# Modulation weights in units of 256 rows by 1024 columns, summed in one bank per vector

## What is computed

```python
def ada_mods(cond, w, b):
    mods = (jax.nn.silu(cond) @ w + b)[..., None, :]
    return jnp.split(mods, ADA_CHUNKS, axis=-1)

sh1, sc1, g1, sh2, sc2, g2 = ada_mods(c, ada_w[i], ada_b[i])
u = modulate(rms_norm(x, mix_pre_g[i]), sh1, sc1)
y = pool_mixer(u, pool_w[j], pool_scale[j])
x = x + g1 * rms_norm(y, mix_post_g[i])
f = conv_ffn(modulate(rms_norm(x, ffn_pre_g[i]), sh2, sc2), ...)
x = x + g2 * rms_norm(f, ffn_post_g[i])
```

## Time and profile before

| | us |
|---|---|
| median of 3 runs | 1162.6 (1162.14 to 1165.11) |
| the profiled execution | 1162.76 |
| its span, first to last instruction | 1161.0 |
| PE busy in it | 1144.4 |

### The profile page before, as it was taken

How to read it: one execution, slowest core, us unless ns; L and a number is a source line. 1 busy time by engine, 2 the same in 40 slices (tenths; PEclk the granted TensorE clock), 3 DMA queues, 4 the chain that set the end, 5 groups by cost and what they waited for, 6 DMA issues and landing times.

```text
span 1161.0 us, 17692 instructions
## 1 busy us (share of the span) xinstructions
PE 1144.4 (99%) x7128; PEld 941.7 (81%) x7128; DVE 564.5 (49%) x908; ACT 495.7 (43%) x655; POOL 444.0 (38%) x336
## 2 busy tenths in 40 slices
PE   9899999999999999999999999999999999999997
PEld 7668888888888888888788888888888888888886
DVE  2572654324451245556986657622110344576835
ACT  4474553544421134774433334554421343534531
POOL 0105554545545451433432311033544535465420
PEclk9999999999999999999999999999999999999999
DMA  9994232332242242223223213013242322323201
GB/s 347 384 385 143 79 108 83 99 108 80 100 130 86 96 141 104 83 73 109 73 74 110 73 37 110 1 37 109 73 156 105 113 78 73 110 74 95 89 1 73
DMA packets 104312, 127.74 MB, mean 110 GB/s; under 512 B 13251, under 2 KB 90801, under 8 KB 104117
## 3 DMA queue, kind: packets, MB, share of 16 engines
q1 hardware_dynamic: 99138, 119.62, 31.1%
q10 hardware_dynamic: 5107, 7.16, 1.8%
HBM read 121.53 MB, written 5.24 MB: 109 GB/s over the span
## 4 chain that ended last, share of the span: by engine, by line
PE 93%; DVE 4%; ACT 2%; issue 1%; POOL 0%; DVEq 0%; ACTq 0%; POOLq 0%
PE ps L273 25%; PE ps L275 24%; PE ps L274 24%; PE ps L1715 3%; PE ps L1741 2%; PE ps L2177 1%; PE ps L2258 1%; PE ps L2264 1%; PE ps L1721 1%; PE ps L2259 1%; PE ps L1784 1%; PE ps L1771 1%; PE ps L2240 1%; PE ps L1992 1%; PE ps L2379 1%
## 5 line engine op out<-in xcount | busy, mean ns | idle before, releaser
L407 POOL TENSOR_TENSOR wl<-raw,wh 128x512 fp32r<-128x512 f32 x312 | 422.8, 1387 | 636.6 <-ACT wh L444 636.6
L273 PE MATMUL ps<-xth,wh 128*128 128x512 f32 (+1 forms) x832 | 325.4, 391 | 0.8 <-DVE xtl L1115 0.6
L275 PE MATMUL ps<-xth,wl 128*128 128x512 f32 (+1 forms) x832 | 317.6, 382 | 0.0
L274 PE MATMUL ps<-xtl,wh 128*128 128x512 f32 (+1 forms) x832 | 317.3, 381 | 0.0
L444 ACT ACTIVATE wh<-raw 128x2048 fp32r<-128x2048 f32 x78 | 149.3, 1914 | 299.0 <-PE ps L275 279.4
L273 PEld LDWEIGHTS ps<-xth,wh 128*128 128x128 f32 x832 | 156.5, 188 | 34.4 <-issue 4.8
L275 PEld LDWEIGHTS ps<-xth,wl 128*128 128x128 f32 x832 | 156.4, 188 | 30.7
L274 PEld LDWEIGHTS ps<-xtl,wh 128*128 128x128 f32 x832 | 156.7, 188 | 28.3 <-issue 0.5
L1123 DVE SCALAR_TENSOR_TENSOR conv_out<-ps,conv_taps,conv_out 128x511 f32<-128x511 f32 x44 | 32.7, 744 | 122.6 <-ACT conv_out L609 122.6
L1218 DVE SCALAR_TENSOR_TENSOR conv_v<-ps,gdn_taps,conv_v 128x511 f32<-128x511 f32 (+2 forms) x96 | 71.8, 748 | 28.9 <-ACT conv_v L677 26.2
L273 PE MATMUL ps<-wh,xth 128*128 128x512 f32 x176 | 69.7, 396 | 0.1
(11 more groups left out here) (341 smaller groups left out, 1668.4 us busy)
## 6 DMA issues: line engine op xcount, KB each, us to landing
ada<-in_ada_w SPq DMA_DIRECT2D x24, 1024.0 KB, 10.9
raw<-in_gdn_w_in SPq DMA_DIRECT2D x24, 1024.0 KB, 5.2
raw<-in_ffn_w_up SPq DMA_DIRECT2D x22, 1024.0 KB, 4.9
raw<-in_gla_w_in SPq DMA_DIRECT2D x12, 1024.0 KB, 5.1
raw<-in_ffn_w_down SPq DMA_DIRECT2D x11, 1024.0 KB, 4.8
raw<-in_gdn_w_out SPq DMA_DIRECT2D x8, 1024.0 KB, 4.8
raw<-in_gla_w_out SPq DMA_DIRECT2D x4, 1024.0 KB, 4.9
xres<-in_x SPq DMA_DIRECT2D x4, 512.0 KB, 5.3
```

The lines of the kernel that those rows point to most:

```text
L273: nc.tensor.matmul(o, lh, rh, start=first, stop=False)
L274: nc.tensor.matmul(o, lh, rl, start=False, stop=False)
L275: return nc.tensor.matmul(o, ll, rh, start=False, stop=last)
L407: rest = nc.gpsimd.tensor_tensor(lo[:, part], raw[:, s, part], hi[:, part].bitcast(f32), ALU.subtract)
```

## The change

A unit now holds 256 rows of 1024 columns: `[128 partitions, 2 row blocks, 1024 columns]`, pieces of 4 KB. Each unit adds to all 1024 columns of its vector, so a vector is complete after its fourth unit and not before. PE makes four matmuls of 512 columns for a unit: row block b and column half h go to column group 2b + h, all in one bank, which is j % 2. So partitions 0 and 64 hold the partial sums of the left half, 32 and 96 those of the right half, and `group_rows` gets two columns that select them. One copy of the bank (`ada_sum`) takes the place of two; `ada_part` holds two vectors in turn. For j = 3 ACT makes the only copy. The bias row of j = 2 lies as two rows of 512 on partitions 0 and 32 and needs two short transfers. `gate_sum` makes one step of 1024 columns for each row block, 8 instead of 32. `ada_summed` now counts vectors.

```diff
-    ada = at("ada", PH + 50 * KB, [ADA_SLOTS, KD, UC])
+    ada = at("ada", PH + 50 * KB, [ADA_SLOTS, 2, D])
...
-            ada_v = cols(a["ada_w"][0], UC)
+            ada_v = a["ada_w"][0].rearrange("(n b p) (j c) -> j n p b c", b=2, p=P, c=D)
...
-                nc.gpsimd.memset(group_rows[32 * c:32 * c + 1, :], 1.0).then_inc(S("prepared"), 1)
+                nc.gpsimd.memset(group_rows[32 * c:32 * c + 1, c % 2:c % 2 + 1], 1.0).then_inc(S("prepared"), 1)
...
-            act.dma_start(gate_bias[0:1, :], a["ada_b"][:, 2 * D:3 * D]).then_inc(S("post_in"), 16)
+            for half in range(2):
+                c = 2 * D + half * 512
+                act.dma_start(gate_bias[32 * half:32 * half + 1, 0:512], a["ada_b"][:, c:c + 512]).then_inc(S("post_in"), 16)
...
-            act.wait_ge(S("mod_mm"), 3)
-            act.wait_ge(S("ada_summed"), 7)
+            act.wait_ge(S("mod_mm"), 2)
+            act.wait_ge(S("ada_summed"), 3)
             nc.scalar.activation(ada_part[:, 1, :], ps[:, 1, :], ACT.Copy).then_inc(S("ada_summed"), 1)
...
-            def ada_half(j, half, b):
-
-                v.wait_ge(S("ada_used"), 4 * j + 2 * half + 2)
-                if j >= 1:
-                    v.wait_ge(S("mod_mm"), j)
+            def ada_sum(j):
+
+                v.wait_ge(S("ada_used"), 4 * j + 4)
+                if j >= 2:
+                    v.wait_ge(S("mod_mm"), j - 1)
                 if j == 2:
-                    v.wait_ge(S("post_in"), 16)
-                    V.tensor_tensor(ada_part[:, half, :], ps[:, b + half, :], gate_bias[:, half * 512:half * 512 + 512], ALU.add)\
-                        .then_inc(S("ada_summed"), 1)
+                    v.wait_ge(S("post_in"), 32)
+                    V.tensor_tensor(ada_part[:, j % 2, :], ps[:, j % 2, :], gate_bias[:, 0:512], ALU.add).then_inc(S("ada_summed"), 1)
                 else:
-                    V.tensor_copy(ada_part[:, half, :], ps[:, b + half, :]).then_inc(S("ada_summed"), 1)
+                    if j == 4:
+                        v.wait_ge(S("ada_summed"), 4)
+                    V.tensor_copy(ada_part[:, j % 2, :], ps[:, j % 2, :]).then_inc(S("ada_summed"), 1)
...
-            ada_half(2, 0, 0)
             norm("y", 0)
-            ada_half(2, 1, 0)
+            ada_sum(2)
...
-            ada_half(3, 0, 0)
             norm("y", 3)
...
-            ada_half(4, 0, 0)
             mod_col(3, 2, SH2)
-            ada_half(4, 1, 0)
+            ada_sum(4)
...
-                for n in range(4):
-                    u, part = 20 + n, g2_acc[:, n * UC:(n + 1) * UC]
...
+                V.scalar_tensor_tensor(g2_acc[:], ada[:, u % ADA_SLOTS, k % 2, :], c_col[:, k:k + 1], g2_acc[:], ALU.mult, ALU.add)\
+                    .then_inc(S("g2_summed"), 1)
...
-                if n % 2 == 0 and j >= 1:
-                    pe.wait_ge(S("ada_summed"), 2 * (j - 1) + n // 2 + 1)
-                for k in range(KD):
-                    c = 32 * (k % 4)
-                    mm = X.matmul(ps[c:c + 32, b + n // 2, o], c_col[:, k:k + 1].broadcast_to([P, 32]), ada[:, u % ADA_SLOTS, k, :],
-                                  start=(k < 4), stop=(k >= 4))
+                if n == 0 and j >= 2:
+                    pe.wait_ge(S("ada_summed"), j - 1)
+                for b in range(2):
+                    k = 2 * n + b
+                    for half in range(2):
+                        c = 32 * (2 * b + half)
+                        mm = X.matmul(ps[c:c + 32, j % 2, :], c_col[:, k:k + 1].broadcast_to([P, 32]),
+                                      ada[:, u % ADA_SLOTS, b, half * 512:half * 512 + 512], start=(n == 0), stop=(n == 3))
...
+                pe.wait_ge(S("ada_summed"), j + 1)
                 for half in range(2):
-                    pe.wait_ge(S("ada_summed"), 2 * j + half + 1)
-                    mm = X.matmul(ps[:, b + half, :], group_rows[:, 0:1].broadcast_to([P, P]), ada_part[:, half, :], start=True, stop=True)
+                    mm = X.matmul(ps[:, b + half, :], group_rows[:, half:half + 1].broadcast_to([P, P]), ada_part[:, j % 2, :], start=True, stop=True)
```

More of the change, by code:

```diff
@@ L1153, in gate_sum @@
             def gate_sum(k):
-                for n in range(4):
-                    u, part = 20 + n, g2_acc[:, n * UC:(n + 1) * UC]
[L1157 to L1160, removed]
-                        v.wait_ge(S("g2_summed"), 4 * (k - 1) + n + 1)
-                    V.scalar_tensor_tensor(part, ada[:, u % ADA_SLOTS, k, :], c_col[:, k:k + 1], part, ALU.mult, ALU.add)\
-                        .then_inc(S("g2_summed"), 1)
+                u = 20 + k // 2
+                if k == 0:
+                    v.wait_ge(S("g2_bias"), 16)
+                else:
+                    v.wait_ge(S("g2_summed"), k)
+                if k % 2 == 0:
+                    v.wait_ge(ada_full[u % ADA_SLOTS], 16 * (u // ADA_SLOTS + 1))
+                V.scalar_tensor_tensor(g2_acc[:], ada[:, u % ADA_SLOTS, k % 2, :], c_col[:, k:k + 1], g2_acc[:], ALU.mult, ALU.add)\
+                    .then_inc(S("g2_summed"), 1)
             with v.Fori(0, 2) as i:
@@ L1750, in mod_col @@
                     for c in range(0, P, 32):
-                        mm = X.matmul(ps[c:c + 32, b, n:n + 1], ada_part[:, half, k * P + c:k * P + c + 32], group_rows[:, 0:1],
+                        mm = X.matmul(ps[c:c + 32, b, n:n + 1], ada_part[:, j % 2, k * P + c:k * P + c + 32], group_rows[:, half:half + 1],
                                       start=True, stop=True)
@@ L1824, in _ @@
                 pool_block(cb)
-            ada_unit(0, 2, 0)
-            ada_unit(0, 3, 0)
+            ada_unit(0, 2)
+            ada_unit(0, 3)
             for cb in range(4, KD):
@@ L1837, in _ @@
             mixed(0)
-            ada_unit(2, 0, 0)
-            ada_unit(2, 1, 0)
-            ada_unit(2, 2, 0)
-            ada_unit(2, 3, 0)
+            ada_unit(2, 0)
+            ada_unit(2, 1)
+            ada_unit(2, 2)
+            ada_unit(2, 3)
             pe.wait_ge(S("mods_done"), 2)
@@ L1845, in _ @@
             mixed(2)
-            ada_unit(3, 0, 0)
+            ada_unit(3, 0)
             mixed(3)
-            ada_unit(3, 1, 0)
-            ada_unit(3, 2, 0)
-            ada_unit(3, 3, 0)
+            ada_unit(3, 1)
+            ada_unit(3, 2)
+            ada_unit(3, 3)
             turn_normed(0)
@@ L1888, in _ @@
             pe.wait_ge(S("mods_done"), 5)
-            pe.wait_ge(S("ada_summed"), 10)
+            pe.wait_ge(S("ada_summed"), 5)
             up_units(0)
```

30 lines of the change are left out of this document (14 added, 16 removed).

## The result

The changed kernel takes 1168.35 us (median of 5 runs, 1166.68 to 1169.7), the kernel before 1162.6 (5 runs, 1162.14 to 1165.11): a ratio of 1.0048, interval 1.0036 to 1.0061, 5.7 us slower. The forecast was 1163.4 and the range ended at 1165.9. The profiled execution of the changed kernel took 1167.97 us, 5.2 more than that of before.

A forecast was written before the change was run, and what follows sets the result against it. The prediction took PE to bound the kernel (99% busy), before 87 us by order and latency; terms -0.19, 0, +0.9 and +0.14 sum to +0.85, on 1162.6 giving 1163.4 us, range 1161.2 to 1165.9.

The forecast's parts named there:

- the one on SP: SP's weight stream: fewer descriptors per unit, SP held less, issue still waiting for PE to free a slot; nothing more.
- The clock rival: PE's low-clock window near 15 us disappears or one more comes: 1161.7 or 1165.1 us, chance 0.06.
- Transfers, -0.19: Weight stream: 4 KB pieces land sooner and save PE's 0.19 us wait for unit 19; bounds 0 and -0.2.
- PE's products, 0: Products with the weights: half the records, twice as wide, take the same time; bounds +0.2 and -0.3 us.
- fixed-cost rival: PE's matmuls: 160 fewer records save a fixed cost each, 2.2 us in all, giving 1161.2 us; chance 0.08.
- (a): Gate row, j = 2: both products wait behind the only copy, so g1_row starts later: +0.9 us (0.85 to 0.95).
- (b): Scale columns, j = 1: all 64 small records wait behind the copy: +0.14 us, bounds 0 and +0.4.
- (c): j = 3: ACT copies the whole, PE's columns wait for it, but earlier norm work offsets this: 0, bounds 0 and +0.4.
- (d): j = 4: the only copy ends before PE wants it: 0, bounds 0 and +0.1 us.
- (e): j = 0, PE's removed waits on ada_summed and ACT's second short gate_bias transfer: no cost or gain, 0.
- (f): g2 steps on DVE: 10.4 us instead of 12.8, where PE waited for nobody, so 0.
- the stream falls behind: Weight stream: 4 KB reads run slower, unit 19 comes late; at 10% slower 1168.6 us; chance 0.05.

The follow-up runs named there:

- e3_two_units: The changed kernel, with SP issuing two units and then waiting for ACT's small rows before the third: 1166.38 us.
- e1_hold: The changed kernel, with SP waiting for ACT's small rows before it issues the first unit: 1162.19 us.
- e2_small_pieces: The changed kernel, with the first six units loaded in pieces of 1 KB, four transfers each, into the new layout: 1163.09 us.
- e5_filler: The changed kernel, with 19 instead of 14 filler matmuls at the start: 1165.26 us.
- e6_short_unit12: The kernel before, with only row blocks 0 to 3 of unit 12 loaded, so the stream behind it is shorter: 1162.77 us.
- e9_shifted_stream: The kernel before, with 32 tiny one-column matmuls behind the fillers, shifting every later instruction against the instruction blocks: 1165.23 us.
- e7_old_j2: e1_hold, with the four units of j = 2 loaded, multiplied and copied in the old way with two half copies: 1161.45 us.
- e4_before_gap: The kernel before, with 7 instead of 14 filler matmuls, so PE is idle ahead of the transposes: 1165.31 us.

## Why the prediction was wrong, point by point

**The step that failed** is the one on SP, which put the effect of larger pieces on everyone else at nothing: "SP issues fewer descriptors per unit and is held less; the issue of unit u still waits for ada_used of unit u-6 ... Nothing more." It looked at when units are issued and at what the stream gives PE, not at who else is in the engines. In the changed kernel SP begins the issue of its sixth unit at 6.8 us; in the kernel before the third is held for 7.06 us and the sixth begins at 18.6. The early issue alone isn't it (e3_two_units); what counts is that each of SP's packets is now four times as large, and from 9 to 10.9 us ACT's queue got 163 packets where it had 286. ACT's rows landed 2.56 us later and its bands 3.5. The prediction's sum had no term for the first 20 us at all; the earlier trace rows shows in its first line that the engines were full there (a share of 1.02 from 5 to 9 us), and full engines with two queues in them were the sign. That came to 1.85 us of late work and, by the clock, 3.2 more. e1_hold and e2_small_pieces take back the whole loss or nearly so.

**The clock rival** had the right place and a wrong premise: "PE does the same up to there in both kernels, so I expect it again". PE doesn't, since it starts its work when data lands. Its price of 1.7 us for 3.4 us more at half speed was right by size: 6.8 us more at the lower level cost 3.2 up to the first product. e5_filler takes away all 10.2 us at that level and wins 4.3 there, of which 3.1 are left at the end, since PE then waits for ACT.

**Transfers, -0.19:** the term was mis-sized and its cause only part of the story. The stretch won 0.8 us: a hole went that goes with a block fetch and not with unit 19 (e6_short_unit12, e9_shifted_stream), and unit 19 also came early enough not to take the hole's place. That 4 KB pieces run faster was right: 400 to 419 GB/s in the windows of 13.4 to 27 us, where the 1 KB ones had 384 to 388. Both are above the 358 GB/s that the prediction took from the Trainium skill, "DMA: Bandwidth & Descriptors", section Bandwidth, as a core's share of HBM.

**PE's products, 0:** right within its bounds. 16 records of 512 columns take 1.92 us, 32 of 256 took 1.93 (e9's row above), and the stretches up to j = 1 gave back 0.18. The fixed-cost rival with its 2.2 us falls. The lower bound of this term was reckoned wrong: half of 0.14 us in each of nine stretches is 0.63 and not 0.3 (and the trace has eight stretches). The stated range doesn't hang on it.

**(a) +0.9:** right, 0.90 in the changed kernel and again by e7_old_j2. **(b) +0.14:** 0.17, from the copy's start to that of L1062. It is the 64 small matmuls in one piece behind the copy, 42.52 to 43.23. **(c), (d), 0:** right. ACT's copy of j = 3 runs from 74.14 to 74.74 and the columns start at 75.03 behind transposes, without a wait; those of j = 4 at 81.32, 0.2 us after their copy's end.

**(e) 0:** the second gate_bias transfer shows no cost; but its words, "ACT's queue ... in a place where ACT next waits for PE's first transposes", name the very wait that grew (6.5 us instead of 4.4), and I took it as cover without asking what ends it.

**(f) 0:** right. The g2 steps of DVE, half of them:

```profile
140.26 5.24 DVE L1160 SCALAR_TENSOR_TENSOR g_acc<-ada,c_col,g_acc 128x1024 f32<-128x1024 f32 x4
```

10.5 us instead of 12.8, and no gain in time.

The remaining rivals (the stream falls behind, the column groups no longer overlap, the change does nothing) fell; the first gave its 1168.6 for another reason than the one that came. With the late data (1.85) and the clock (3.2) added and the stretch at 74 us at -0.8 for -0.19, the sum reads 1162.6 + 0.9 + 0.14 - 0.8 + 1.85 + 3.2 = 1167.9; the median is 1168.35.

## What to carry to other kernels

Where two queues are in full DMA engines, the one with the larger packets can hold up the other, as it did here: before making a bulk stream's pieces larger, look at which small loads land beside it and what starts with them, and hold the stream back until they are in. An engine's first real work hangs on such loads, and a gap of some 2 us ahead of it can cost more in clock than in waiting (3.2 us against 1.85). Before giving a hole of "issue" inside a run of matmuls to a semaphore, see whether one can stand there at all; and look at what lands just behind the hole, since that wait will take its place.

## What the runs showed of the hardware

- Two queues on the same 16 DMA engines were served at near equal counts of packets from 9 to 12 us, whether SP's packets had 1 or 4 KB (245 to 242; 333 to 406; 296 to 320). From 5 to 7 us they were not (213 to 39).
- A gap of 1.8 us in PE's work near the start was followed by 6.8 us at the lower clock, gaps of 2.6 and 2.7 us by 10.2, one of 0.5 us, or none, by 3.4. Two runs stand apart: with 19 fillers and no gap there was no low stretch in the start at all, and with 2.1 us of one-column matmuls in place of a gap it was 6.8 us. So it isn't idle time alone that counts; what decides isn't settled.
- PE had holes of 0.6 to 1.8 us (from start to start of two records) that ended 2.2 to 2.4 us after a fetch of a 16 KB instruction block started, while the DMA engines were full of weights. The Trainium skill, "Runtime: NRT & Kernel Launch", section Instruction fetch mechanics, has the blocks of 16 KB and calls their cost mostly hidden. In the kernel before five of seven left no hole that shows and one of the other two cost little; the one at 74 us was not hidden. That the fetch is the cause is inferred from the times, from the hole's move by 14 records in e4_before_gap and from e9_shifted_stream; no run takes the fetch away.
- 64 records of tiny matmuls, one column each and all on the same column group, took 2.12 us, 33 ns each; the 64 of `mod_col`, spread over groups by fours, took 0.71, 11 ns each. They differ in their operands too, and no run changes the group alone.
